# Two transformer blocks on one core: 72 more products at the kernel's end, with stepped and narrow weights

## The chip, the cores and the metric

The kernel runs on one core of one Trainium2 chip (trn2). The metric is the device time of one execution, in microseconds (us); several runs of the same program are given by their median. The names of the engines are those of the profile: PE is TensorE (PEld its weight loads), DVE is VectorE, ACT is ScalarE, POOL is GpSimd and SP is SyncE, which issues most of the DMA transfers.

## The reference

The reference takes x of 512 tokens and 1024 features through three layers, all in float32: a mixer of compressed, selected and windowed attention beside a pooling branch, with a gated feed-forward layer; a convolution module with a second feed-forward layer; then a gated linear attention with a short convolution, a third feed-forward layer and a gated per-layer embedding (`ple`). Only the very end matters here:

```
u3 = _rmsnorm(h, ln3_g[i])
gate = jax.nn.sigmoid(u3 @ w_ple_gate[i])
h = h + gate * (p[i] @ w_ple_proj[i])
...
return _rmsnorm(h, lnf_g)
```

The final norm divides each token by the root of the mean of its squares over the 1024 features and scales each feature by a gain.

## The kernel before, in words

Activations lie transposed in SBUF: the 128 partitions hold 128 features of one of eight tiles (`KD` = 8), the free dimension the 512 tokens (`S`). A matrix product of float32 accuracy is made of three matmuls of type float32r, whose operands are split into a high and a low part: high times high, high times low and low times high (`mm3`, lines 1104 to 1106). `act_hi` and `act_lo` are the two parts of the activations, each [128, 8, 512]; the weights of a panel stand, split likewise, in `w0` or `w1`, of 48 + 2 x 2048 elements a partition each, of which the first 48 (`SKEW`) lie ahead of the panel. A matmul names the weights first and the moving operand second; for each the machine issues a weight load and a matmul.

The work of each engine is written out by hand as one program per engine, in the order in which it runs, with semaphores between them: no scheduler moves anything. The program of PE is the function under `@block.tensor`. The feed-forward layers use products of 256 columns (line 1454) and, in the down projection, products that read `hid_hi` and `hid_lo` through `halves` (line 207): that view takes the columns 0, 256, 1, 257 and so on, so that two neighbouring columns of the product come from places 256 elements apart. The compressed attention has a stream of products of 124 columns (lines 1215 and 1216), and the layer norm of the convolution module has products of one column (line 1565, `add_tokens`), with `src` as the weights and a column of ones as the moving operand; behind them stand `spread_mean` (line 1582) and `repeat_rstd` (line 1179).

The end of PE's program, ahead of which nothing changes:

1. The last panels of `ple`, products of 512 columns.
2. `add_to_sums` (line 1781) sums the squares of seven feature tiles over the partitions, four matmuls with one column each; the profile shows two machine instructions for each of them, since they are of plain float32.
3. `TAIL_WARM` = 8 products (line 1788) of 512 columns go into `ps[6]`, which nobody reads.
4. When ACT has squared the last tile of x (semaphore `sq_ready`), `add_to_sums` adds it. ACT takes the root (line 662), DVE the reciprocal (line 1850).
5. `repeat_rstd(5)` (line 1179) waits for that (`tok_inv`) and spreads the factor of each token over all partitions, into `ps[5]`, with four matmuls (eight machine instructions). It signals `rstd_repeated`, and PE's program ends.

DVE waits for `rstd_repeated` and multiplies x by the gain and by `ps[5]` in nine pieces (line 2634, `OUT_PIECES`: the first tile in two halves, then seven tiles), each followed by a signal `y_ready`. SP waits for each signal, issues the transfer of the piece to HBM (line 444) and at last waits for all nine transfers. The block's end, where each engine drains its queue and all meet, is recorded under line 133.

Of the kernel before, what the change touches and what calls it, by code (L numbers as in the profile page):

```python
# [25 lines left out]
P = 128  # L26
# [5 lines left out]
SKEW = 48  # L32
# [6 lines left out]
HALF = S // 2  # L39
# [91 lines left out]
def program(nc, t):  # L131
    ctx = ExitStack()
    with ctx:
        def sb(name, shape, dt=F32):
            return ctx.enter_context(nc.sbuf_tensor(name, shape, dt))
# [25 lines left out]
        w1 = sb("w1", [P, SKEW + 2 * SLOT], F32R)  # L161
        act_hi = sb("act_hi", [P, KD, S], F32R)
        act_lo = sb("act_lo", [P, KD, S], F32R)
# [41 lines left out]
        def halves(v):  # L205

            return v.rearrange("p (h c) -> p c h", h=2)
# [8 lines left out]
        def flat(v):  # L216
            return v.rearrange("p k n -> p (k n)")
# [84 lines left out]
        ps = [ctx.enter_context(nc.psum_tensor(f"ps{i}", [P, S], F32)) for i in range(8)]  # L302
# [798 lines left out]
        def _(pe):  # L1101
# [73 lines left out]
            def repeat_rstd(count, src=tok_rstd, dst=5):  # L1175

                pe.wait_ge(sem("tok_inv"), count)
                for b in range(TB):
                    ins = pe.matmul(ps[dst][:, b * P:(b + 1) * P], src[:, b:b + 1].broadcast_to([P, P]),
                                    ident[:, :], start=True, stop=True)  # L1180
                ins.then_inc(sem("rstd_repeated"), 1)
# [608 lines left out]
            add_to_sums(sq[:, 1], False).then_inc(sem("sumsq"), 1)  # L1790
            repeat_rstd(5)


        @block.vector
        def _(ve):
# [929 lines left out]
```

## Time and profile before

| | |
|---|---|
| Median of 3 runs | 1687.73 us |
| Lowest and highest | 1687.16 and 1688.9 us |
| The profiled execution | 1688.09 us |
| Its span, first to last instruction | 1686.3 us |
| Mean granted TensorE clock | 0.996 |
| Matmuls / weight loads in the trace | 10716 / 10716 |
| Output | 9 transfers, 2.10 MB in all |

The span is what the views of the trace count in: times in them start at the span's first instruction. The profiled execution takes 1.8 us more than its span. A line number is that of the kernel's source; work recorded in a helper has the helper's line. "Idle before" is the time that an engine stood still ahead of a group, with the instruction that ended it behind an arrow. Durations of matmuls are modelled and overlap, as do those of weight loads, so the distance between two starts says more of the pace than a duration does. The granted clock is given as a share of TensorE's full 2.4 GHz.

### The profile page before, as it was taken

How to read it: one execution, taken by the hardware profiler on the slowest of the kernel's cores; microseconds unless marked ns; L12 is line 12 of the kernel's file. 1: busy time of each engine (PE TensorE's matmuls, PEld its weight loads, DVE VectorE, ACT ScalarE, POOL GpSimd, SP SyncE). 2: the span in 40 equal slices, each digit the busy share in tenths (PEclk: the TensorE clock that was granted, in tenths of full speed). 3: DMA queues.
4: the chain of work that ended last, by engine and by line, in shares of the span. 5: the costliest groups of instructions: out<-in, count | busy, mean ns of one | idle time of the engine just before them, and what ended most of it. 6: DMA issues, size and time to landing. Idle time of an engine off the chain costs nothing.

```text
span 1686.3 us, 27591 instructions
## 1 busy us (share of the span) xinstructions
PE 1664.0 (99%) x10716; PEld 1461.9 (87%) x10716; DVE 1259.2 (75%) x1752; ACT 854.7 (51%) x1314; POOL 527.4 (31%) x368
## 2 busy tenths in 40 slices
PE   9989999999999999999999999999999999999997
PEld 7867789999998866789999998788888999899886
DVE  7767788845876798788855887688868975488675
ACT  6448457724763322557733774433335673277342
POOL 1451125503540446326502540121502560255000
PEclk9999999999999999999999999999999999999999
DMA  6310223433433565223344333422222333433432
GB/s 223 91 51 2 76 75 105 115 113 94 119 105 104 130 153 141 81 75 101 102 114 112 101 107 97 132 75 75 76 76 75 101 101 113 113 101 92 121 94 81
DMA packets 284923, 169.11 MB, mean 100 GB/s; under 512 B 8336, under 2 KB 278880, under 8 KB 284800
## 3 DMA queue, kind: packets, MB, share of 16 engines
q1 hardware_dynamic: 283792, 165.16, 34.8%
q8 instruction: 84, 1.38, 0.4%
q0 software_dynamic: 720, 1.72, 0.3%
q10 hardware_dynamic: 288, 0.54, 0.1%
q14 instruction: 39, 0.32, 0.1%
HBM read 156.71 MB, written 2.10 MB: 94 GB/s over the span
## 4 chain that ended last, share of the span: by engine, by line
PE 50%; DVE 4%; ACT 1%; issue 1%; DVEq 0%; ACTq 0%
PE ps L1454 22%; PE ps L1104 9%; PE ps L1106 9%; PE ps L1105 9%; DVE w L1803 1%; PE ps L1668 1%; ACT w L640 1%; DVE w L2131 0%; DVE act_lo L1835 0%; DVE bt_lo L1833 0%; DVE rstd L1845 0%; DVE tt L2147 0%; ACT w L810 0%; DVE x L2634 0%; PE ps L1681 0%
## 5 line engine op out<-in xcount | busy, mean ns | idle before, releaser
L1104 PE MATMUL ps<-act_hi,w 128*128 128x512 f32 x788 | 312.8, 397 | 3.8 <-DVE w L1803 2.3
L1106 PE MATMUL ps<-act_hi,w 128*128 128x512 f32 x788 | 307.0, 390 | 0.0
L1105 PE MATMUL ps<-act_lo,w 128*128 128x512 f32 x788 | 306.9, 390 | 0.0
L1454 PE MATMUL ps<-act_hi,w 128*128 128x256 f32 (+1 forms) x1461 | 270.3, 277 | 1.6 <-DVE w L2131 1.1
L640 ACT ACTIVATE w<-raw 128x2048 fp32r<-128x2048 f32 (+2 forms) x102 | 163.1, 1599 | 193.6 <-PE ps L1106 179.7
L1454 PEld LDWEIGHTS ps<-act_hi,w 128*128 128x128 f32 x1461 | 229.2, 188 | 3.3 <-DVE w L2131 1.7
L1803 DVE TENSOR_TENSOR w<-raw,w 128x2048 fp32r<-128x2048 f32 (+2 forms) x93 | 180.8, 1944 | 41.4 <-ACT w L640 41.3
L477 POOL TENSOR_TENSOR raw<-raw 128x512 f32<-128x512 f32 x60 | 81.9, 1365 | 405.4 <-DVE sqacc L1823 164.0
L1104 PE MATMUL ps<-hid_hi,w 128*128 128x512 f32 x528 | 200.1, 379 | 0.0
L1105 PE MATMUL ps<-hid_lo,w 128*128 128x512 f32 x528 | 200.1, 379 | 0.0
L1106 PE MATMUL ps<-hid_hi,w 128*128 128x512 f32 x528 | 200.1, 379 | 0.0
L1454 PE MATMUL ps<-act_lo,w 128*128 128x256 f32 x720 | 199.3, 277 | 0.0
L1104 PEld LDWEIGHTS ps<-act_hi,w 128*128 128x128 f32 x788 | 147.9, 188 | 45.2 <-issue 7.5
L1106 PEld LDWEIGHTS ps<-act_hi,w 128*128 128x128 f32 x788 | 147.9, 188 | 31.4
L1105 PEld LDWEIGHTS ps<-act_lo,w 128*128 128x128 f32 x788 | 148.0, 188 | 30.5 <-issue 1.2
L2131 DVE TENSOR_TENSOR w<-raw,w 128x2048 fp32r<-128x2048 f32 x60 | 147.7, 2462 | 19.9 <-ACT w L810 18.9
L487 POOL TENSOR_TENSOR raw<-raw,ssum 128x512 f32<-128x512 f32 x60 | 99.2, 1653 | 178.4 <-DVE w L2131 178.4
L2137 DVE TENSOR_TENSOR sw_lo<-ps,sw_hi 128x512 fp32r<-128x512 f32 x180 | 122.8, 684 | 31.7 <-ACT ps L824 31.4
L1454 PEld LDWEIGHTS ps<-act_lo,w 128*128 128x128 f32 x720 | 135.5, 188 | 0.4
L1454 PE MATMUL ps<-bt_hi,sw_hi 128*128 128x256 f32 x480 | 133.0, 277 | 0.0
L1454 PE MATMUL ps<-bt_hi,sw_lo 128*128 128x256 f32 x480 | 132.8, 277 | 0.0
L1454 PE MATMUL ps<-bt_lo,sw_hi 128*128 128x256 f32 x480 | 132.8, 277 | 0.0
(430 smaller groups left out, 3595.6 us busy)
## 6 DMA issues: line engine op xcount, KB each, us to landing
raw<-in_ffn_w_gate_dram SPq DMA_DIRECT2D x44, 512.0 KB, 4.0
raw<-in_ffn_w_up_dram SPq DMA_DIRECT2D x44, 512.0 KB, 5.2
raw<-in_w_gate_upffn_dram SPq DMA_DIRECT2D x44, 512.0 KB, 4.5
raw<-in_ffn_w_down_dram SPq DMA_DIRECT2D x32, 384.0 KB, 4.2
raw<-in_conv_w_pw_dram SPq DMA_DIRECT2D x24, 512.0 KB, 5.7
raw<-in_w_in_dram SPq DMA_DIRECT2D x24, 512.0 KB, 4.4
raw<-in_ffn_w_down_dram SPq DMA_DIRECT2D x32, 320.0 KB, 3.7
z<-z SPq DMA_DIRECT2D x30, 262.0 KB, 4.9
```

The lines of the kernel that those rows point to most:

```text
L477: pool.tensor_tensor(r[:, 2], r[:, 2], r[:, 3], ALU.add).then_inc(sem("w_sums"), 1)
L487: pool.tensor_tensor(r[:, 1], r[:, 1], ssum[:, 0], ALU.subtract).then_inc(sem("w_sums"), 1)
L640: act.activation(w_of(n)[0][:, 0:cols], raw[:, n % 2, 0:cols], ACT.Copy).then_inc(hi_done, 1)
L1104: pe.matmul(out, lhs[0], rhs[0], start=start, stop=False)
L1105: pe.matmul(out, lhs[0], rhs[1], start=False, stop=False)
L1106: return pe.matmul(out, lhs[1], rhs[0], start=False, stop=stop)
L1454: ins = pe.matmul(out[:, c], lhs, rhs[:, k, c], start=start and k == 0 and rhs is b_hi and lhs is w_hi, stop=k == Q4 - 1 and lhs is w_lo, ...
L1668: ins = pe.matmul(out, kd[part, o:o + P], right, start=True, stop=True)
L1803: ve.tensor_tensor(w_lo[:, a], raw[:, n % 2, a], w_hi[:, a].bitcast(F32), ALU.subtract)\
L2131: ve.tensor_tensor(w_lo, raw[:, n % 2], w_hi.bitcast(F32), ALU.subtract)\
L2137: ve.tensor_tensor(sw_lo[:, c], sum_bank(dn, c)[:, :], sw_hi[:, c].bitcast(F32), ALU.subtract)\
```

## The change

Behind `repeat_rstd(5)`, at the very end of PE's program, 72 products are added. Each takes weights of 128 partitions and, in most cases, 128 columns, multiplies them with the first 64 or 256 columns of `act_hi[:, i]` (read through `halves`, so that two neighbouring columns come from places 32 or 128 elements apart), and writes the result to `ps[6]`, as an accumulation group of its own. Nobody reads it, nothing is waited for, nothing signalled. They come in groups of three, i = 0, 1, 2, whose weights start 128 elements apart. For 64 columns and then for 256, the groups are, in this order: weights as they are in `w1`; weights from `act_lo` with a step of 1, 2, 4, 8, 16, 17 and 20 elements (4 bytes each) between two columns; 96, 112 and 124 neighbouring columns of `w1`; and again 128 columns of `w1`. That makes 12 groups, or 36 products, for each of the two column counts.

```diff
--- before.py
+++ after.py
@@ -1789,6 +1789,27 @@
             pe.wait_ge(sem("sq_ready"), 8 * OUT + 8)
             add_to_sums(sq[:, 1], False).then_inc(sem("sumsq"), 1)
             repeat_rstd(5)
+
+            def unread(weights, columns, times=3):
+                for i in range(times):
+                    w = weights(SKEW + i * P)
+                    pe.matmul(ps[6][0:w.shape[1], 0:columns], w, halves(act_hi[:, i, 0:columns]), start=True,
+                              stop=True)
+
+            def stepped(step):
+                v = flat(act_lo[:, :, :])
+                return lambda at: v[:, at - SKEW:at - SKEW + P * step:step]
+
+            def as_is(at):
+                return w1[:, at:at + P]
+
+            for columns in (64, HALF):
+                unread(as_is, columns)
+                for step in (1, 2, 4, 8, 16, 17, 20):
+                    unread(stepped(step), columns)
+                for wide in (96, 112, 124):
+                    unread(lambda at: w1[:, at:at + wide], columns)
+                unread(as_is, columns)
 
 
         @block.vector
```

The output and all that leads to it are unchanged.

## Rows read from the trace of the kernel before

**Rows 1.** The page: span, engines, TensorE clock in 40 slices

```profile
span 1686.3 us, 27591 instructions
...
PE 1664.0 (99%) x10716; PEld 1461.9 (87%) x10716; DVE 1259.2 (75%) x1752; ACT 854.7 (51%) x1314; POOL 527.4 (31%) x368
...
PEclk9999999999999999999999999999999999999999
```

**Rows 2.** Timeline, 1655 to 1687 us: start, duration, engine, line, operation

```profile
1676.97 1.16 PE L1179 MATMUL ps<-ident,wtap 128*128 128x128 f32 x8 [0.57 <-DVE wtap L1850]
1678.17 5.48 DVE L2634 SCALAR_TENSOR_TENSOR x<-x,par,ps 128x256 f32<-128x256 f32 x9 [1.25 <-PE ps L1179]
```

**Rows 3.** Waits of SP, from 1670 us: total, times, longest

```profile
SPq L133 <- DMA out_dram<-x: 1.9, 1, 1.9
```

**Rows 4.** Line 133: durations ns min/median/max, first and last start

```profile
L133 PEldq DRAIN  x1: 1187/1187/1187, 1677.0 to 1677.0; - x1
...
L133 SPq DRAIN  x1: 7/7/7, 1686.1 to 1686.1; - x1
```

**Rows 5.** Timeline of PE, 674 to 692 us: products of one column

```profile
681.61 1.03 PE L1565 MATMUL ps<-ones,sqacc 128*128 128x1 f32 x8
682.50 1.03 PE L1565 MATMUL ps<-ones,zc 128*128 128x1 f32 x8
```

**Rows 6.** Timeline of PE, 43.5 to 48.5 us: products of 124 columns

```profile
43.90 0.27 PE L1215 MATMUL ps<-cmp,w 128*128 128x124 f32 x1
...
47.03 0.28 PE L1215 MATMUL ps<-cmp,w 128*128 128x124 f32 x1
```

**Rows 7.** Timeline of PE, 251.0 to 252.3 us: products of 256 columns

```profile
251.04 0.28 PE L1454 MATMUL ps<-act_hi,w 128*128 128x256 f32 x1
...
252.29 0.28 PE L1454 MATMUL ps<-act_hi,w 128*128 128x256 f32 x1
```

**Rows 8.** Weight loads by form: count | busy us, mean ns | idle

```profile
L1104 PEld LDWEIGHTS ps<-act_hi,w 128*128 128x128 f32 x788 | 147.9, 188 | 45.2 <-issue 7.5 <-DVE w L1803 5.2 <-POOL w L559 1.7
...
L1549 PEld LDWEIGHTS ps<-z,diag 128*32 128x32 f32 x256 | 7.5, 109 | 17.5 <-issue 17.5
L1368 PEld LDWEIGHTS ps<-ident,rg 128*64 128x64 f32 x128 | 7.0, 136 | 0.9 <-issue 0.7
```

**Rows 9.** Timelines, 400 to 401.5 us (read in halves) and from 1655 us

```profile
400.06 0.38 PE L1105 MATMUL ps<-hid_lo,w 128*128 128x512 f32 x1
...
401.36 0.38 PE L1105 MATMUL ps<-hid_lo,w 128*128 128x512 f32 x1
...
1655.06 0.39 PE L1104 MATMUL ps<-act_hi,w 128*128 128x512 f32 x1
...
1657.10 0.39 PE L1104 MATMUL ps<-act_hi,w 128*128 128x512 f32 x1
```

**Rows 10.** Groups of DVE by form: count | busy us, mean ns | idle

```profile
L1823 DVE TENSOR_TENSOR sqacc<-sqacc,sq 128x512 f32<-128x512 f32 x55 | 37.9, 689 | 15.5 <-ACT sq L646 14.0 <-DVE x L2159 0.8
...
L1898 DVE TENSOR_TENSOR acc<-acc,par 128x248 f32<-128x248 f32 x8 | 4.2, 589 | 0.5 <-ACT acc L688 0.5
...
L1975 DVE TENSOR_TENSOR s_sb<-s_sb,cmx 128x1024 f32<-128x1024 f32 x1 | 1.2, 1224 | 0.0
```

**Rows 11.** Busy time by stretch (columns in the first row)

```profile
core 0: us, PE busy (x) PEld busy (x) DVE busy (x) ACT busy (x) POOL busy (x), PEclk, DMA share, GB/s
...
45.50:46.50 1.00, 1.00 (x12) 1.00 (x10) 1.00 (x1) 1.00 (x2) 1.00 (x2) 1.00 0.09 16
...
683.00:684.00 1.00, 1.00 (x10) 1.00 (x11) 0.33 (x2) 0.00 (x0) 0.00 (x0) 0.93 0.00 0
684.00:685.00 1.00, 1.00 (x5) 1.00 (x6) 0.06 (x1) 0.00 (x0) 0.00 (x0) 0.50 0.06 16
...
690.00:691.00 1.00, 1.00 (x4) 0.62 (x2) 0.78 (x2) 0.97 (x3) 1.00 (x2) 0.65 0.00 0
```

**Rows 12.** Timeline of PE's weight loads, 685 to 692 us

```profile
686.33 1.83 PEld L1179 LDWEIGHTS ps<-ident,wtap 128*128 128x128 f32 x8
```

## The prediction

> **What bounds the kernel now.** I read the page first. PE is busy in 99% of the span, at a granted clock of 1.00 nearly throughout [rows 1]; the change adds PE work alone, so the question is whether anything after it on PE has to wait, or whether something else ends the kernel. So next the timeline of the last 14 us. PE's last work, eight matmuls that repeat the token factors, starts at 1676.97 and ends at 1678.14 us [rows 2]. From there DVE scales x in nine pieces from 1678.17 for 5.48 us, SP sends each piece to HBM, and its last wait is for the last output transfer, 1.9 us [rows 3]. The records of the end of the program (line 133) show what is left: the drain of PE's queue starts at 1677.0 and takes 1.187 us, so it is done at 1678.19, 0.05 us after the last matmul; SP drains at 1686.1 [rows 4] and the span ends at 1686.3 [rows 1]. So PE is idle and nobody waits for it from 1678.19 to 1686.1: a cover of 7.9 us. The new products write ps[6], which nobody reads afterwards, have no wait and give no signal, and stand behind the matmuls that release DVE. They delay no one but the end of the program: they cost nothing up to the cover and all of what exceeds it.
>
> **The change, part by part.** Nothing is removed or moved. Added are 2 x 36 = 72 pairs of a weight load and a matmul. Of the 36 with one column count, 12 read 128 weight columns densely or nearly so (three each for as_is at the start, as_is at the end, step 1 and step 2), 15 read with a step of 4, 8, 16, 17 or 20 elements, 9 load 96, 112 or 124 columns.
> *Full width, 64 columns.* Not in the trace; bounds from both sides. Of the products of one column in the middle of the kernel a group of eight starts at 681.61 us and the next at 682.50: 0.111 us each [rows 5]. A stream of 124 columns has its 3rd start at 43.90 and its 31st at 47.03: 28 intervals, 0.112 us each [rows 6]. Both ends are the same, so the load of the weights sets the pace. I take 0.112.
> *Full width, 256 columns.* Starts from 251.04 to 252.29 us, 11 intervals between them: 0.113 us each [rows 7].
> *Narrower loads.* A load of 128 columns lasts 188 ns, of 64 columns 136, of 32 columns 109 [rows 8]: (188-136)/64 = 0.81 and (136-109)/32 = 0.84 ns a column. So 96, 112 and 124 columns save 26, 13 and 3 ns each where the load sets the pace, which for 64 columns is 3 x 42 ns = 0.13 us; for 256 columns the matmul alone needs about half of the 0.227 us between two starts with 512 columns (1655.06 to 1657.10, 9 intervals [rows 9]), 0.113, so nothing is saved. The bounds are 0 and that 0.13 us.
> *Sum if steps are free.* 36 x 0.112 - 0.13 = 3.90 us and 36 x 0.113 = 4.07 us, together 7.97. The last old matmul starts about 0.28 us before its end at 1678.14, the first new one 0.112 us later, at 1677.97. The last new one starts at 1677.97 + 7.97 - 0.11 = 1685.83, ends 0.28 later, and the queue is drained at 1686.16. SP drained at 1686.1. So even then the cover is used up to the last tenth: +0.05 us.
> *Steps of 4 and more elements (16 bytes and more).* No weight load in the trace reads with such a step, so I bound it. From below: the products of the down projections read their moving operand in halves, alternating between places 256 elements apart, and start every 0.22 us (400.06 to 401.36 in 6 intervals, 0.217), faster than the 0.227 us of the contiguous ones [rows 9]. PE's read of the moving operand thus jumps on each element at no cost; by this row a step costs 0, the lower end. From above: on DVE, 248 elements read with a step of 16 elements take 589 ns in the mean; 512 contiguous ones take 689 ns and 1024 take 1224 [rows 10], so (1224-689)/512 = 1.04 ns each plus 154 ns fixed, by which 248 would take 413. The step adds 176 ns, 0.71 ns an element: each costs 1.75 ns in place of 1.04. If a weight column can't come faster than that either, 128 columns need 224 ns in place of 107 (128 x 0.84), and each stepped product takes 0.117 us more than a dense one, about twice the time. I take exactly twice, 0.107 more, since DVE's elements cost 1.7 times, not more than double. For the steps 4 to 20 that is 30 products (two sets of 15) x 0.107 = +3.2 us; by 0.117 it would be +3.5. With a step of 2 there are two elements in every 16 bytes, and I take it as dense. Between the ends I take the upper one: the DVE row has what matters, every element from another place and none near it used soon after, while in halves each place is followed by its neighbour two elements later, which a small buffer could serve. A weight load is also a plain one-pass read, as DVE's is.
> The Trainium skill, page "SBUF — State Buffer", section "Door 1: The DMA port swizzle", says that SBUF has lines of 16 bytes and full bandwidth needs at least two hits per line, each access to a new line paying a penalty. By its wording, that consecutive accesses must hit the same line, the products in halves would be slower than the contiguous ones; the trace does not agree: 0.217 against 0.227 us. [...] The Trainium skill's page "TensorE: Matmul & The Clock Gate", section "LDWEIGHTS (loading the stationary operand)", speaks against the forecast: it gives a load's time as its column count over 1.2 GHz and names no step. By that the sum is the +0.05 us, which is the first rival below; of the dense loads the trace agrees, with 0.112 us from start to start.
> *The clock.* The granted clock fell once inside the kernel: products of one column ran from 680.70 us, at 1.00 (2.4 GHz) until the slice 683 to 684, then at 0.50 (1.2 GHz) until the slice 690 to 691 [rows 11]: by the means of these slices from 683.86 to 690.7 us. At that level eight loads of 128 columns take 1.83 us [rows 12]; with some 0.33 for the last one's own time that is (1.83-0.33)/7 = 0.214 us each. The stream of 124 columns held 1.00 [rows 6, 11]. Products of 64 columns lie between; if the stepped loads take 0.22 us, they stand even farther apart, and their stretch is 3.9 + 1.6 = 5.5 us long. So if steps cost double I expect the fall, about 3.2 us into the stretch as in the row, near 1681.2 us, in the middle of the stepped loads. A stepped product then costs nothing more (0.214 is below 0.22); the 12 products behind them cost 0.214 in place of 0.10 to 0.11, +1.3 us; if the level lasts 6.8 us as in the row, the first 9 of 256 columns add 9 x 0.10 = 0.9. That makes +1.3 to +2.2.
> *Forecast.* 0.05 + 3.2 + 1.3 = +4.5 us. The profiled execution is 1688.09 us with its span of 1686.3; the median of the three runs is 1687.73. On the median: 1692.2 us; on the profiled execution 1692.6. The output transfers and DVE's pieces keep their times. What a measurement can tell from no change is 0.2%, 3.4 us.
>
> **Rivals.**
> *Steps are free (the other side).* Place: the 30 stepped loads; price 0. For it: the products in halves [rows 9]; against it: the DVE row [rows 10]. Time 1687.8, no change. It decides from 0 to about 0.11 us a stepped load: at 0.11 the sum reaches the 3.4 us. Chance 37%.
> *Steps cost double, but the clock holds.* For it: 1.00 under 124 columns [rows 11], and the products of 256 columns soon fill the array. Time +3.25 us, 1691.0, just under the bound. 19%, of which 6 would read as slower.
> *Steps free, clock falls all the same.* The 64-column stretch is then 3.9 us long; +1.3 to 2.5 us, 1689 to 1690.2. 4%.
> *Some step is worse than double.* A step of 16 elements could meet the same place of the memory each time. The DVE row is of this very step and shows 1.7 times [rows 10], which speaks against it. If six loads took 0.43 us, +1.3 us on the forecast: 1693.5. 4%.
> *The change does nothing.* Unread products that start an accumulation run in the kernel already, the eight of line 1788, and nothing takes them out. I give it nothing.
>
> **How the numbers follow.** The forecast (double, with a fall of the clock) has 36%. Slower by over 0.2%: 36 + 6 + 4 = 46%. Within: 13 + 36 + 4 = 53%. Faster: 1%, noise around the case of free steps. Both kinds hold much, so the forecast's own range is 1691.6 (stepped loads at 1.9 times) to 1693.4 (the longer fall, +2.2, and 0.05 + 3.2). The range must reach to the free steps at 37%: from 1687.2, the lowest run shown, to 1693.6.
>
> **What would show it.** The new line's loads in the profile: starts 0.112 us apart for as_is, step 1 and 2 and about 0.22 us for steps 4 to 20 with both column counts; 0.085 to 0.108 for the narrow ones with 64 columns only; a granted clock of 0.50 from about 1681; SP drained at 1686.1 as before and PE's drain last, near 1690.6. I am wrong if steps 4 to 20 start 0.112 us apart (then the time stays), if the clock is 1.00 to the end (then about 1691), or if the last transfer lands later than 1686.

## The result, and the profile after

The changed kernel takes 1694.82 us in the median of 8 runs (1691.62 to 1697.51), beside 1688.93 us (1687.16 to 1690.65) in 8 runs of the kernel before: 1.0036 times as long [1.0025, 1.0047], or 5.9 us more. The forecast was 1692.2 us, and the range ended at 1693.6. The profiled execution takes 1696.84 us, with a span of 1695.1. The page of the changed kernel has the 72 added matmuls; the slices of the clock show nothing new at their coarseness:

```profile
span 1695.1 us, 27735 instructions
...
PE 1678.7 (99%) x10788; PEld 1475.2 (87%) x10788; DVE 1258.7 (74%) x1752; ACT 853.2 (50%) x1314; POOL 528.0 (31%) x368
...
PEclk9999999999999999999999999999999999999999
```

The difference between the two profiled spans, 8.8 us, is two things. The chain that ended last shows where the old work of PE ends:

```profile
1680.19 1.16 PE ps L1179 x8
1681.35 13.46 PE ps L1796 x72
```

The eight matmuls of the token factors end at 1681.35 us, against 1678.13 before [rows 2]: 3.2 us of the difference lie ahead of the first added product, in work that the change doesn't touch. From the factors' end to the end of the span it is 1695.1 - 1681.35 = 13.7 us, against 1686.3 - 1678.13 = 8.2 us; with the unrounded ends 13.71 and 8.18, so +5.53 us. I call this stretch the tail. It is the effect of the change, and it agrees with the medians' 5.9.

The records of line 133, which answer to [rows 4], and SP's waits, which answer to [rows 3], show that the output is as it was and that PE ends last (first line 133, then the waits from 1670 us on):

```profile
L133 SPq DRAIN  x1: 7/7/7, 1689.3 to 1689.3; - x1
L133 PEldq DRAIN  x1: 2867/2867/2867, 1692.0 to 1692.0; - x1
```
```profile
SPq L133 <- PEq L133: 5.7, 1, 5.7
SPq L133 <- DMA out_dram<-x: 1.9, 1, 1.9
```

SP drains 8.0 us behind the factors' end, as before (1678.13 to 1686.1), its last output transfer still takes 1.9 us of waiting, and then it waits 5.7 us for PE.

In the timeline, a group with 21 products is the seven steps, those with 15 and 12 are narrow and dense ones between and behind them (columns: start, duration, engine, line, operation):

```profile
1681.44 4.30 PE L1796 MATMUL ps<-act_hi,act_lo 128*128 128x64 f32 x21
...
1685.56 3.29 PE L1796 MATMUL ps<-act_hi,w 128*96 128x64 f32 x15
...
1688.64 4.86 PE L1796 MATMUL ps<-act_hi,act_lo 128*128 128x256 f32 x21
...
1693.34 1.48 PE L1796 MATMUL ps<-act_hi,w 128*96 128x256 f32 x12
```

From 1681.44 to 1685.56 the 21 stepped products of 64 columns take 4.12 us, where the sum of free steps has 21 x 0.112 = 2.35. Looked at one by one, their starts are 112 ns apart for a step of 1, 118 for 2, 233 for 4, 238 for 8, 217 for 16, 221 for 17 and 235 for 20. With 256 columns the larger steps show the same, 220 to 245 ns, but for the first of them (213) and one of 186 where the clock rises again. The dense and the narrow ones with 256 columns, at the end, start 109 to 112 ns apart. But those between 1685.56 and 1688.64 stand farther apart than they should: 161 ns for 96 weight columns, 187 for 112, 207 for 124 and 213 for 128. The busy time by stretch answers to [rows 11], with the same columns (the granted clock is the third number from the end):

```profile
1683.00:1684.00 1.00, 1.00 (x6) 1.00 (x6) 1.00 (x2) 0.00 (x0) 0.00 (x0) 1.00 0.77 263
1684.00:1685.00 1.00, 1.00 (x6) 1.00 (x6) 1.00 (x3) 0.00 (x0) 0.00 (x0) 0.67 1.03 383
1685.00:1686.00 1.00, 1.00 (x7) 1.00 (x7) 1.00 (x2) 0.00 (x0) 0.00 (x0) 0.50 1.02 377
...
1691.00:1692.00 1.00, 1.00 (x7) 1.00 (x6) 0.00 (x0) 0.00 (x0) 0.00 (x0) 0.91 0.00 0
...
1237.00:1238.00 1.00, 1.00 (x8) 1.00 (x7) 1.00 (x3) 0.98 (x3) 0.00 (x0) 0.60 0.00 0
...
1244.00:1245.00 1.00, 1.00 (x8) 0.84 (x7) 0.00 (x0) 0.00 (x0) 0.00 (x0) 0.99 0.00 0
```

By the means of the slices the clock is at 0.50, its lower level of 1.2 GHz, from 1684.34 to 1691.18 us, 6.8 us as in [rows 11], beginning 3.0 us behind the factors' end. And it was there from 1237.2 to 1244.0 us too, in the head norm, where the profile of before has no fall. PE's timeline of that stretch, first of the kernel before, then of the changed one:

```profile
1236.64 1.93 PE L1738 MATMUL ps<-ones,la 128*128 128x1 f32 x16
...
1240.79 0.39 PE L1105 MATMUL ps<-act_lo,w 128*128 128x512 f32 x1
```
```profile
1236.70 3.11 PE L1738 MATMUL ps<-ones,la 128*128 128x1 f32 x16
...
1244.06 0.40 PE L1105 MATMUL ps<-act_lo,w 128*128 128x512 f32 x1
```

The sixteen products of one column start within 0.06 us of each other in the two kernels, and the same product of line 1105 behind them starts at 1240.79 and at 1244.06. Less the 0.06, this fall costs 3.2 us, and that is the 3.2 us ahead of the added products.

### The profile page after: what moved, and what is told of

The parts are those of the page before. It is cut to its first block, busy times and chain, and to the rows that moved or that the text cites. A ratio compares the mean times of both kernels' runs of the same rounds, so it can differ in the third digit from the quotient of the medians.

```text
span 1695.1 us, 27735 instructions
## 1 busy us (share of the span) xinstructions
PE 1678.7 (99%) x10788; PEld 1475.2 (87%) x10788; DVE 1258.7 (74%) x1752; ACT 853.2 (50%) x1314; POOL 528.0 (31%) x368
## 4 chain that ended last, share of the span: by engine, by line
PE 51%; DVE 4%; ACT 1%; issue 1%; DVEq 0%; ACTq 0%
PE ps L1454 21%; PE ps L1104 9%; PE ps L1106 9%; PE ps L1105 9%; PE ps L1796 1%; DVE w L1824 1%; PE ps L1668 1%; ACT w L640 1%; DVE w L2152 1%; ACT w L810 0%; DVE act_lo L1856 0%; DVE bt_lo L1854 0%; DVE rstd L1866 0%; DVE tt L2168 0%; PE ps L1738 0%
```

## The experiments

Two questions were open. Is the tail's +5.5 us the sum that the forecast names (stepped loads at twice the pace, and a fallen clock for the rest), or another? And what is a stepped load's price a function of: does any step cost double, and is it the weight load's alone? Most kernels are edits of the changed one (the last three are edits of the kernel before), and each one's profile, which is of one execution, gives the tail by itself, which the variation of the rest of the kernel doesn't touch. Kernels that were run together share their runs of the kernel before. I write f for the end of the factors' matmuls.

**All 72 weights dense.** If steps cost nothing, or the clock matters more than they do, this shows it.

```diff
             for columns in (64, HALF):
-                unread(as_is, columns)
-                for step in (1, 2, 4, 8, 16, 17, 20):
...
-                unread(as_is, columns)
+                for group in range(12):
+                    unread(as_is, columns)
```

> All 72 products read dense weights of 128 columns (12 groups of 3 for 64 and for 256 columns); no step, no narrow load. Theory (steps of 4 and more elements double the load, and the clock falls under the long stretch of 64 columns): starts 0.112 us apart throughout, PE done near SP's drain, no more than +0.5 us on the kernel before, ratio 1.000, clock 1.00 until the last matmul. Rival (the count of instructions or the 64-column stretch alone costs, steps do not): +4 us or more, as in the changed kernel.

Measured: 1693.52 us (11 runs; before 1688.11, 31 runs), ratio 1.0022 [1.0013, 1.0031]. (The quotient of the two medians is 1.0032; single runs of this kernel go from 1688.57 to 1695.67 us.) The tail is 13.2 us, +5.0 on the kernel before: all dense it is only 0.5 us shorter than with 30 stepped ones. The stretches of its profile say why:

```profile
1680.00:1681.00 1.00, 1.00 (x13) 1.00 (x11) 0.95 (x3) 0.00 (x0) 0.00 (x0) 1.00 0.00 0
1681.00:1682.00 1.00, 1.00 (x8) 1.00 (x8) 1.00 (x2) 0.00 (x0) 0.00 (x0) 0.65 0.47 157
1682.00:1683.00 1.00, 1.00 (x6) 1.00 (x6) 1.00 (x3) 0.00 (x0) 0.00 (x0) 0.50 0.88 314
1690.00:1691.00 1.00, 1.00 (x7) 1.00 (x6) 0.00 (x0) 0.00 (x0) 0.00 (x0) 0.50 0.00 0
1691.00:1692.00 1.00, 1.00 (x9) 1.00 (x9) 0.00 (x0) 0.00 (x0) 0.00 (x0) 0.73 0.00 0
```

While the clock is 1.00, 13 instructions fall into the microsecond; from 1681.3 us, 1.3 us behind f = 1680.0, it is 0.50 for 10.2 us, and 6 or 7 fit: 213 ns each. So a dense load at the lower level costs what a stepped one costs at either. The expectation of a clock that holds is refuted: what PE did ahead of this fall, behind the factors' eight matmuls, was 1.5 us of products of 64 columns, 0.112 us apart, with dense weights (they begin at 1679.8). Steps are not needed for it. What stands ahead of f (products of one column, a wait of 0.6 us, the factors' products) is the same in every kernel here; whether it has a part in the fall is taken up with wide72.

**256 columns first, then 64.** In the dense kernel the fall came in the part with 64 columns; the order moves that part.

```diff
-            for columns in (64, HALF):
+            for columns in (HALF, 64):
```

> The same 72 products, the 36 of 256 columns first. If the fall of the clock costs what the dense and narrow products lose under it, then here it falls late, inside or behind the 64-column stretch: dense products of 256 columns run at 0.113 us, stepped ones at 0.22 to 0.24 as before; +3.5 to +4.2 us on the kernel before, 1.5 to 2 us less than the changed kernel. Rival (the fall costs nothing, the steps cost all): the same time as the changed kernel within 0.5 us.

Measured: 1692.25 us (11 runs; before 1688.11), ratio 1.0022 [1.0013, 1.0031]. The tail is 12.8 us, +4.6. The clock is at 1.00 through the products of 256 columns and falls at 1688.92, 9.8 us behind f = 1679.1, when the products of 64 columns, which begin at 1684.8, have run for 4 us. Two stretches around it:

```profile
1688.00:1689.00 1.00, 1.00 (x6) 1.00 (x6) 0.00 (x0) 0.00 (x0) 0.00 (x0) 0.96 0.00 0
1690.00:1691.00 1.00, 1.00 (x6) 1.00 (x7) 0.00 (x0) 0.00 (x0) 0.00 (x0) 0.50 0.00 0
```

The products are the same 72; in this order the clock falls later and spares 0.9 us of the tail. That is less than the 1.5 to 2 us expected, and neither side of the expectation is borne out: the late fall still lies over the narrow and dense products of 64 columns, which start 161 to 214 ns apart.

**256 columns throughout.** If the products of 64 columns bring the fall about, this kernel has the price of the steps alone.

```diff
-            for columns in (64, HALF):
+            for columns in (HALF, HALF):
```

> Both halves with 256 columns: 72 products in the same patterns of weights. Theory: the clock stays at 1.00, stepped products start 0.22 to 0.24 us apart, the others 0.109 to 0.113 (narrow ones too): 30 x 0.23 + 42 x 0.11 = 11.5 us, +3.6 us on the kernel before. Rival (the clock falls because of the stepped loads, not of the few columns): a granted clock of 0.50 within the products and +5 us or more.

Measured: 1692.76 us (9 runs; before 1688.11), ratio 1.0026 [1.0016, 1.0036]. The tail is 11.9 us, +3.7, and the clock is at its full level to the end, through stepped and dense ones alike, as two of its stretches show:

```profile
1679.00:1680.00 1.00, 1.00 (x6) 1.00 (x6) 1.00 (x2) 0.00 (x0) 0.00 (x0) 1.00 0.48 161
...
1684.00:1685.00 1.00, 1.00 (x10) 1.00 (x9) 0.00 (x0) 0.00 (x0) 0.00 (x0) 1.00 1.04 387
```

By the forecast's working, with 72 x 0.113 for free steps and 30 x 0.117 for the steps (the dearer of its two prices), it should be +0.2 + 3.5 = +3.7. So the price of the steps stands by itself, and what 64 columns for the first half add to the tail is 5.5 - 3.7 = 1.8 us. The work ahead of f is as in dense72, and here nothing fell behind it: by itself it doesn't bring the fall about. Whether it helps where products of 64 columns follow isn't shown.

SP's last output transfer was a little later here and in swapped, and cost nothing, since PE ends last. SP's wait, the same in both:

```profile
SPq L133 <- DMA out_dram<-x: 2.3, 1, 2.3
```

**The part with 64 columns alone.** A kernel that uses half of the cover.

```diff
-            for columns in (64, HALF):
+            for columns in (64,):
```

> Only the 36 products of 64 columns. They end by 1678.0 + 5.5 = 1683.5 us on the time line of before, or by 1686 if the clock falls, under the cover of DVE's pieces and the output transfers: no change (ratio 1.000, within 0.1%). Rival (stepped reads of PE slow DVE's pieces or the transfers): DVE's last piece or SP's drain later than before by more than 0.3 us against the factors' end.

Measured: 1687.85 us (11 runs; before 1688.11), ratio 1.0000 [0.9991, 1.0009]. The tail is 8.2 us, as before. PE is drained at 1679.8 + 3.9 = 1683.7, behind f = 1677.0 by 6.7 us, and SP ends, as the records of line 133 show:

```profile
L133 PEldq DRAIN  x1: 3853/3853/3853, 1679.8 to 1679.8; - x1
...
L133 SPq DRAIN  x1: 7/7/7, 1685.0 to 1685.0; - x1
```

The clock fell here too, 3.5 us behind f, and it cost nothing: these 36 products fit under the output transfers whatever their pace.

**Dense and 256 columns throughout.** Neither steps nor 64 columns: by the sum the cover should just hold it.

```diff
             for columns in (64, HALF):
...
+            for columns in (HALF, HALF):
+                for group in range(12):
+                    unread(as_is, columns)
```

> 72 dense products of 128 weight columns, all of 256 columns: neither steps nor the 64-column stretch. Theory (steps and the fall of the clock are the only two costs, and the kernel with dense weights and 64 columns was slow through the fall alone): 72 x 0.112 = 8.1 us, clock 1.00 to the last product, end of the program no more than 0.3 us later against the end of the factors than before, ratio 1.000 within 0.1%. Rival (72 more products cost something by themselves, such as their instructions): +2 us or more.

Measured: 1690.02 us (11 runs; before 1687.97, 21 runs), ratio 1.0014 [1.0005, 1.0023]. Its tail is 9.9 us, +1.7, where no more than 0.3 was expected. PE is drained at 1682.9 + 2.2 = 1685.1, f = 1677.0 + 8.1, as expected, with the clock at 1.00. But PE isn't last. SP's waits from 1670 us on:

```profile
SPq L133 <- DMA out_dram<-x: 3.6, 1, 3.6
SPq L133 <- PEq L133: 0.2, 1, 0.2
```

and a line of its DMA queues from 1683 to 1685 us (packets, MB, share of the 16 engines):

```profile
q8 instruction: 1, 0.02, 3.0%
```

SP's wait for its last output transfer is 3.6 us in place of 1.9 [rows 3]; the transfer lands 9.1 us behind f in place of 7.4. In the microseconds of the output a transfer of 16 KB runs on the queue that brings instructions (q8), 6.5 us behind f, 0.97 us long; neither the kernel before nor half64 has one behind f. The packets of the output show what is late: sixteen of 2 KB each end one after the other from 7.65 to 9.06 us behind f, while in the kernel before the last packet ends at 7.38. The changed kernel has the transfer of code as well, 8.5 us behind f, when the output has landed (7.4) and only PE is left. In swapped and wide72 it is recorded at 7.7 us, and the last output packet ends there, 0.3 us late.

**The dense products in a loop.** If that transfer of code delays the output, the same 72 products from a short loop, which need no more code than 12 of them, should give the time back.

```diff
             for columns in (64, HALF):
...
+            with pe.Fori(0, 6) as i:
+                for group in range(4):
+                    unread(as_is, HALF)
```

> The 72 dense products of 256 columns again, as a loop of 6 passes over 12 products. Theory (the kernel with all of them written out was 2 us slower because the longer program needs one more block of code, 16 KB, fetched at 6.5 us after the factors' end, while the output transfers run, and the last transfer then landed 1.7 us later): no fetch behind the factors, SP's drain 7.97 us after the factors' end as before, PE done at about the same time plus the loop's own time, ratio 1.000 within 0.1%. Rival (72 products that fill PE delay the transfers or DVE themselves): SP's drain 1.7 us late again.

Measured: 1689.38 us (12 runs; before 1689.2, 23 runs), ratio 1.0002 [0.9991, 1.0012]. The tail is 8.3 us. PE's drain ends at the same place, 8.1 us behind f; no transfer of instructions follows f. SP's waits from 1670 us on show 1.9 us again:

```profile
SPq L133 <- DMA out_dram<-x: 1.9, 1, 1.9
SPq L133 <- PEq L133: 0.3, 1, 0.3
```

So 1.6 us of the tail of the dense kernel were the output's, not PE's. The cover of 7.9 us is as the forecast had it, as long as no code is brought in during the transfers.

**Only the 30 stepped products.**

```diff
             for columns in (64, HALF):
-                unread(as_is, columns)
-                for step in (1, 2, 4, 8, 16, 17, 20):
+                for step in (4, 8, 16, 17, 20):
                     unread(stepped(step), columns)
...
```

> Only the 30 products whose step is 4 or more. 30 x 0.23 = 6.9 us from 0.2 us before the factors' end: PE done at 7.0 us behind it, under the cover of 7.97. Theory (what a stepped load costs is paid only beyond the cover): no change, ratio 1.000 within 0.1%, SP's drain as before. Rival (stepped reads of PE also slow the output transfers or DVE's pieces, which read and write the same memory): SP's drain late by 0.3 us or more.

Measured: 1687.64 us (12 runs; before 1689.2), ratio 0.9994 [0.9985, 1.0003]. The tail is 8.2 us. PE is drained at 1680.2 + 4.5 = 1684.7, 7.0 us behind f = 1677.7: thirty products of about 0.23 us each. The clock falls at f + 3.4 us here too, and for half of the stepped products it is 0.50, with no change of their pace (six in a microsecond in both of these stretches):

```profile
1680.00:1681.00 1.00, 1.00 (x6) 1.00 (x6) 1.00 (x2) 0.00 (x0) 0.00 (x0) 1.00 0.88 327
...
1683.00:1684.00 1.00, 1.00 (x6) 1.00 (x6) 0.23 (x1) 0.00 (x0) 0.00 (x0) 0.50 1.00 373
```

**The changed kernel again**, unaltered, run together with the two before.

> The changed kernel once more, unaltered, beside the two above. Theory: between the factors' end and the program's end 13 to 14 us where the kernel before has 8.13, of which the stepped loads make 30 x 0.117 = 3.5 and the fall of the clock 1.5 to 2.5; median 5 to 6 us over the kernel before. The fall may begin anywhere from 1.3 to 5 us behind the factors, and so the tail may differ by 1 us between executions. Rival: a tail that is the same to 0.2 us with the fall elsewhere.

Measured: 1695.73 us (5 runs; before 1689.2), ratio 1.0041 [1.0025, 1.0056]. Its tail is again 13.7 us, but the clock fell 1.0 us behind f and stayed down for 10.2 us. So the expectation's rival holds, the same tail with the fall elsewhere: where the clock falls varies, and the 3.4 us more of the lower level lay over stepped loads, which keep their pace under it.

**One pattern of weights after another.** The 72 products are replaced by 20 groups of four products of 64 columns, each group with weights of another pattern, between which three products of 512 columns stand.

```diff
...
+            lo_ = flat(act_lo[:, :, :])
+            for step, first_at, wide in ((1, 0, P), (1, 1, P), (1, 2, P), (2, 0, P), (2, 1, P), (3, 0, P), (4, 0, P), ...):
+                full()
+                w = lo_[:, first_at:first_at + wide * step:step]
+                for _ in range(4):
+                    pe.matmul(ps[6][0:wide, 0:64], w, act_hi[:, 0, 0:64], start=True, stop=True)
...
```

> In place of the 72 products, groups of four products of 64 columns, one pattern of weights each, with three products of 512 columns between groups to keep the clock at 1.00. Theory (a weight column from a line of 16 bytes of its own costs two array cycles more, whatever the step): starts 0.112 us apart for steps 1 and 2 whatever the first element, between 0.112 and 0.22 for step 3 (three elements in four lines), 0.22 to 0.24 for steps 4, 5, 6, 8, 12, 16, 24, 28; half of that for 64 columns with step 4; 0.85 ns a column saved for 124, 112, 96 and 64 dense columns. Rival (the memory's banks set it): step 5 or 6 near 0.112, or 12, 24, 28 apart from 8 and 16 by over 0.03 us.

Measured (one run, 1709.72 us; its time is that of 143 long and short products and says nothing). In the timeline each pattern's group (L1804) is followed by the group of 512 columns (L1795). From one start to the other are three intervals and 0.03 us for the distance of the first two starts, so one product takes (difference - 0.03) / 3:

```profile
1681.38 0.53 PE L1804 MATMUL ps<-act_hi,act_lo 128*128 128x64 f32 x4
1681.74 0.94 PE L1795 MATMUL ps<-act_hi,w 128*128 128x512 f32 x3
...
1684.81 0.55 PE L1804 MATMUL ps<-act_hi,act_lo 128*128 128x64 f32 x4
1685.19 0.94 PE L1795 MATMUL ps<-act_hi,w 128*128 128x512 f32 x3
...
1688.45 0.89 PE L1804 MATMUL ps<-act_hi,act_lo 128*128 128x64 f32 x4
1689.18 0.94 PE L1795 MATMUL ps<-act_hi,w 128*128 128x512 f32 x3
...
1706.37 0.55 PE L1804 MATMUL ps<-act_hi,act_lo 128*64 128x64 f32 x4
1706.76 0.94 PE L1795 MATMUL ps<-act_hi,w 128*128 128x512 f32 x3
```

In the order of these pairs: step 1, (0.36 - 0.03) / 3 = 0.11 us; step 2, 0.12; step 4, 0.23; and 64 columns with a step of 4, 0.12. The others: step 3 0.17, steps 5 and 6 0.22, step 8 0.24, 12 0.27, 16 0.22, 24 0.25, 28 0.23, and 64, 96, 112 and 124 neighbouring columns 58, 85, 98 and 108 ns. Where in its 16 bytes the first element lies changes nothing (tried with steps 1, 2 and 4). There is one simple reading, made from these times: a load touches a number of 16-byte places, 32 of them with a step of 1, 64 with 2, 96 with 3, 128 from 4 on, or 64 for 64 columns in a step of 4. Above the dense pace the time is 1.82 ns for each place: 64 give 0.117, 96 give 0.175, 128 give 0.233. So the price rises from a step of 2 to one of 4 and then stays between 0.22 and 0.24, apart from 12 and 24, which I can't explain: they lie 0.05 and 0.03 us above 16 and 0.03 and 0.01 above 8, in part the sign that the expectation gave for its rival, the memory's banks. For steps 5 and 6, which aren't near 0.112, that rival's sign is missing; for these two it stays open. The Trainium skill, page "SBUF — State Buffer", section "Door 1: The DMA port swizzle", has this rule: lines of 16 bytes, two hits in each wanted for full bandwidth. The runs agree for the weights: two hits in each (step 2) 0.118, four 0.112, one 0.23.

**The same for the moving operand.** The 72 products are replaced by 13 groups of four products of 256 columns with dense weights, whose moving operand has another pattern in each.

```diff
...
+            patterns = [lo_[:, 0:HALF * step:step] for step in (1, 2, 3, 4, 5, 8, 12, 16)]
+            patterns += [lo_[:, 0:128 * 8].rearrange("p (a b) -> p a b", b=8)[:, :, 0:2],
+                         lo_[:, 0:64 * 16].rearrange("p (a b) -> p a b", b=16)[:, :, 0:4],
+                         halves(lo_[:, 0:HALF]), ...
...
```

> In place of the 72 products, groups of four products of 256 columns with dense weights, whose moving operand has one pattern each, and three products of 512 columns between groups. Theory (a small buffer served the products in halves, and PE pays for lines as DVE does): steps 1 and 2 at 0.112 us, steps 4 and more at 0.43 us or more (1.67 ns a column), pairs of neighbours 8 apart at 0.11 to 0.22, fours of neighbours and plain halves at 0.11, halves whose elements lie 8 apart slow. Rival (PE's moving read pays nothing for a step, only the weight read does): 0.11 us for every pattern.

Measured (one run, 1699.58 us). Here the time from a pattern's start (L1806) to the next group's (L1795), by four, is the time of a product:

```profile
1678.08 0.63 PE L1806 MATMUL ps<-act_lo,w 128*128 128x256 f32 x4
1678.55 0.85 PE L1795 MATMUL ps<-act_hi,w 128*128 128x512 f32 x3
1679.24 1.09 PE L1806 MATMUL ps<-act_lo,w 128*128 128x256 f32 x4
1680.14 0.87 PE L1795 MATMUL ps<-act_hi,w 128*128 128x512 f32 x3
...
1692.40 0.65 PE L1806 MATMUL ps<-act_lo,w 128*128 128x256 f32 x4
1692.89 0.84 PE L1795 MATMUL ps<-act_hi,w 128*128 128x512 f32 x3
1693.57 0.61 PE L1806 MATMUL ps<-act_lo,w 128*128 128x256 f32 x4
1694.01 0.86 PE L1795 MATMUL ps<-act_hi,w 128*128 128x512 f32 x3
```

Step 1 takes 0.12 us and step 2 already 0.23; four neighbours, with each four 16 elements behind the last, 0.12; halves 0.11. The others, from the same timeline: steps 3, 4 and 5 0.22 to 0.23, 8 and 16 0.22, 12 0.31, pairs of neighbours 8 elements apart 0.23, and halves whose elements lie 8 apart 0.21. The expectation is right for the halves and fails at both ends of the steps: a step of 2 isn't free, and larger ones cost double and not more, 0.9 ns a column. The halves' jumps of 128 elements do cost nothing. For the moving operand the Trainium skill's wording in the same section, that consecutive accesses must hit the same line, fits neither halves nor pairs: by it the halves would pay and the pairs would not, while a product in halves takes 0.11 us and one in pairs 0.23.

**More work in the head norm.** From the runs so far a fall of the clock in the middle of the kernel seemed to set the spread between the runs. In the kernel before, with no added products at the end, two products of 512 columns are put into each of the two inner passes of the head norm's loop (`GH` is 4):

```diff
+                if 0 < h < GH - 1:
+                    for _ in range(2):
+                        pe.matmul(ps[5][:, :], w_of(N0["mix2"])[0][:, 0:P], act_hi[:, 0], start=True, stop=True)
```

> The kernel before, with four unread products of 512 columns between the groups of one-column products of the head norm (line 1738, at 1235 us). Theory: in some runs the clock falls there (in the changed kernel's profile from 1237.2 to 1244.0 us, in that of before not), which spreads the runs of one kernel by 3 us; with the filler it stays at 1.00, the slow end of the runs (1689 to 1690.2) is gone and the median lies up to 1 us lower, the four products costing 0.9 us. Rival (the spread has another cause): the same spread of over 3 us, median up to 0.9 us higher.

Measured: 1689.92 us (11 runs, 1686.49 to 1691.26; before 1687.97), ratio 1.0010 [1.0001, 1.0019]. The median isn't lower; the four products themselves should cost 4 x 0.227 = 0.9 us [rows 9]. The profile is of the fastest run and has no fall near 1237, but six of the 11 runs still had a mean clock of 0.995 as slower runs of the kernel before have. The spread isn't gone, and that this fall alone sets it isn't shown: the expectation isn't borne out, and the question stays open.

The tails side by side, from each kernel's profile: f, how long the clock was down near 683 and near 1237 us, and from f to the end of the span, in us:

| | f | near 683 | near 1237 | tail | against before |
|---|---|---|---|---|---|
| before | 1678.1 | 6.8 | none | 8.2 | |
| changed | 1681.4 | 6.8 | 6.8 | 13.7 | +5.5 |
| changed_again | 1679.3 | none | 6.8 | 13.7 | +5.5 |
| dense72 | 1680.0 | 6.8 | 6.8 | 13.2 | +5.0 |
| swapped | 1679.1 | 3.4 | 3.4 | 12.8 | +4.6 |
| wide72 | 1678.0 | 3.4 | 3.4 | 11.9 | +3.7 |
| dense_wide72 | 1677.0 | 3.4 | 3.4 | 9.9 | +1.7 |
| looped_dense | 1677.6 | 6.8 | none | 8.3 | +0.1 |
| half64 | 1677.0 | 6.8 | none | 8.2 | 0.0 |
| stepped30 | 1677.7 | 6.8 | none | 8.2 | 0.0 |

## Why the prediction was right or wrong

**Both costs were the forecast's, but three sizes were off (the stepped loads, the clock's fall and the base), and the reason given for the fall was wrong.** The forecast's +4.5 us was 0.05 for free steps, 3.2 for the stepped loads and 1.3 for the clock. Measured on the tail it is +5.5, and the base lay 1.2 us higher than taken. Neither alone would have taken the time past the range's end of 1693.6: the forecast's base with +5.5 is 1693.2, and its +4.5 on the base measured is 1693.4.

*The cover of 7.9 us.* Right. SP drained 8.0 us behind f in the changed kernel, with the same 1.9 us of waiting, and the output didn't move. It held because the transfer of code came 8.5 us behind f, when the output had landed. This I had not thought of, so it was luck; dense_wide72 shows that at 6.5 us it costs 1.7 us.

*Dense loads, 0.112 and 0.113 us from start to start.* Right: 112 ns for as_is and step 1 and 109 to 112 with 256 columns. A step of 2, taken as dense, takes 118 ns, 0.006 more. The sum of free steps was a little high all the same: by the forecast's working 72 products at 0.113 end with PE drained 8.2 us behind f, and in dense_wide72 it was 8.06; the first product starts 0.24 us ahead of f, where 0.17 was taken.

*Narrow loads, less time with 64 columns only.* Right in size where the clock was up: 85, 98 and 108 ns for 96, 112 and 124 columns in weight_patterns, which saves 27, 14 and 4 ns against 26, 13 and 3 in the forecast. In the changed kernel they fell under the lower clock and took 161, 187 and 207.

*Stepped loads.* The double was right and its size short. I took "exactly twice", 0.107 more each and +3.2; in the changed kernel the mean is 0.228 us, 0.116 more, and 30 x 0.116 = +3.5. That is nearly the DVE row's own figure, 0.117, which I had rounded down with no row for it [rows 10]. wide72, where the clock stays up, gives the 3.5 by itself.

*The fall of the clock, +1.3.* This is the step that failed, by its size: +2.1 us in place of +1.3. The place came out right, 3.0 us behind f where the forecast had 3.1, but that was luck: in the same kernel run again it was 1.0 us. What was wrong is the length. I took the level to last no longer than the dense and narrow products of 64 columns, and gave only the range the longer one. It lasted the 6.8 us of the row, and the first nine products of 256 columns stood under it, too. The 12 behind the stepped ones took 2.30 us in place of 1.21, +1.1, and the nine +1.05 (0.14 of it the step from 64 to 256 columns): +2.1 us, near the upper end that I had written down. The row that told its length [rows 11] was the same that told its start, and I used one half of it. With the 0.05 of free steps the sum is 0.05 + 3.5 + 2.1 = 5.7, against 5.5 measured; most of the 0.2 is what the sum of free steps had too much.

*Why it falls.* I argued that stepped loads, being slower, bring the fall. dense72 takes that away: products of 64 columns with dense weights had it 1.3 us after f, and it stayed at the lower level for 10.2 us. The clock falls in the kernel before as well, 2.4 us behind f, with PE idle and at no cost:

```profile
1680.00:1681.00 1.00, 0.00 (x0) 0.00 (x0) 1.00 (x3) 0.00 (x0) 0.00 (x0) 0.78 0.83 295
```

So stepped loads aren't needed for a fall here. wide72 and swapped show the other half: with 256 columns the clock stayed up, stepped or dense, in the four profiles where they came first (the other two are dense_wide72 and looped_dense); it fell in all five where 64 came first. What in the products of 64 columns does it, few columns or something that goes with them, isn't shown. So the rival in which the steps are free and the clock falls was priced too low at 1.3 to 2.5 us: dense72 is nearly that kernel (it has no narrow loads, and its fall lasted longer), and its tail is 5.0 us longer. The two costs don't add up: with the clock down, a dense load takes 213 ns and a stepped one 217 to 238. The steps alone cost 3.7 us (wide72), the fall alone 5.0 (dense72), and both together 5.5.

*The rivals.* Free steps: refuted by every start distance. Double with a holding clock: that is wide72, +3.7 in place of the +3.25. Some step worse than double: a step of 8, at 238 ns and up to 245 with 256 columns, is the worst of the changed kernel, little over double; a step of 12, which it doesn't have, takes 0.27. The change does nothing: no.

*The range.* Two of its inner bounds don't follow from the forecast's own terms: stepped loads at 1.9 times give 1692.0, not 1691.6, and the longer fall, 0.05 + 3.2 + 2.2 on 1687.73, gives 1693.2, not 1693.4.

*The base.* The range took the rest of the kernel as fixed at the three runs shown. The kernel before has medians of 1688.93 us in 8 runs, 1688.11 in 31, 1687.97 in 21 and 1689.2 in 23, so the base lies 0.2 to 1.5 us above the 1687.73 of three runs. Single runs of it go from 1685.1 to 1691.6 us, and the mean granted clock orders them: in 31 runs, 1686.36 us on the mean of those at 0.998, 1687.55 at 0.997, 1688.71 at 0.996, 1689.24 at 0.995 and 1689.69 at 0.994. The falls in the body come or don't (the table), and the one near 1237 costs 3.2 us. Whether the falls in the body cause the whole spread stays open, since filled_gn didn't take it away.

So of the miss of 1694.82 - 1692.2 = 2.6 us, 1.2 is the base of these runs, 0.3 the stepped loads and 0.8 the clock, less the 0.2 that the sum of the parts lies above the measured tail; 0.4 is the difference between the medians' +5.9 and the tail's +5.5, within the interval, and 0.1 is rounding.

## What to carry to other kernels

Float32 operands read with gaps run TensorE at half its pace, weights from a step of 4 elements on and the moving operand from a step of 2: lay them out densely where their loads or columns set the pace, and leave them where another wait covers them. Work put on an idle engine behind the last useful instruction is free up to the last transfer's end only if it brings no new code in during the transfers; a loop does that. And where a row shows that a level of the clock is left for so many microseconds, take its whole length into the sum, not only its start, and ask which of the products under it lose by it. Last, a median of three runs was 1.2 us off here: give the base a width of its own.

## What the runs showed of the hardware that I had not expected

- A weight load's time fits 1.82 ns for each 16-byte place that it touches, once this exceeds the dense pace: 0.117 us for 64 places, 0.174 for 96 and 0.233 for 128 (weight_patterns). The steps 4, 8, 16, 17 and 20 take 0.22 to 0.24 us at 1.00 and at 0.50 alike. A step of 12 (0.27) and one of 24 (0.25) lie above and are not explained.
- A moving operand of 256 columns pays from a step of 2 on (0.23 against 0.12 us), and in pairs; in fours or in halves it doesn't.
- Behind the same work ahead of f, products of 64 columns with dense weights, 0.112 us apart, had the granted clock fall after 1.5 us (dense72); products of 256 columns at the same distance held 1.00 in wide72 and dense_wide72 to the end.
- A fall lasts 3.4, 6.8 or 10.2 us in these profiles, and what a fall costs goes from nothing (half64, under the cover) to 3.2 us (6.8 us of it over dense products near 1237).
- 16 KB of code brought in during the output's transfers held the last of them up by 1.7 us at 6.5 us behind f (dense_wide72) and by 0.3 us at 7.7 (wide72, swapped), and cost nothing behind them.
